# A fused two-layer attention and expert kernel: the output projection as seven block products

## The reference

```python
mixed = (gates[:, :, 0] * (out_a @ w_o_nsa[l]) + gates[:, :, 1] * (out_b @ w_o_mla[l])
         + gates[:, :, 2] * (out_c @ w_o_fox[l]))
x = x + mixed.astype(x.dtype) @ w_out[l]                 # [256,1024] @ [1024,1024]
x = x + hier_moe(rmsnorm(x, norm_ffn[l]), ...)           # logits, top group, top 2 experts, gate/up/down
```

## Time and profile before

| | us |
|---|---|
| three runs, median | 1014.33 |
| lowest, highest | 1013.62, 1015.16 |
| the profiled execution | 1014.46 |
| its span, first to last instruction | 1012.5 |
| TensorE busy in it | 936.8 (93%) |
| VectorE, ScalarE busy | 383.2, 241.6 |
| mean granted TensorE clock | 0.971 |

### The profile page before, as it was taken

The page is one execution under the profiler, slowest core; times in us unless marked ns, Lnnn a source line. Parts: engine busy times, 40 slices in busy tenths (PEclk is TensorE's granted clock), DMA queues, the critical chain, the costliest instruction groups (busy, mean ns, idle before and its releaser), DMA issues. The chain is left out here.

```text
span 1012.5 us, 14003 instructions
## 1 busy us (share of the span) xinstructions
PE 936.8 (93%) x5512; PEld 638.8 (63%) x5512; DVE 383.2 (38%) x1034; ACT 241.6 (24%) x682; POOL 78.6 (8%) x121
## 2 busy tenths in 40 slices
PE   9999999999999998677899999999999999986676
PEld 8888778775586543334288887887747855532342
DVE  2523676774633211111131337677565321100112
ACT  1211454552111020000111015655411202000002
POOL 0300000114000000000020000000220000000000
PEclk9999999999999998898999999999999999987899
DMA  9985655439989999999998443436398999999995
GB/s 291 299 271 143 139 168 160 167 99 316 333 353 361 421 420 421 422 421 421 359 311 268 130 149 111 143 100 220 122 358 310 351 402 417 420 422 420 421 415 186
DMA packets 137191, 295.14 MB, mean 291 GB/s; under 512 B 14158, under 2 KB 101412, under 8 KB 115620
## 3 DMA queue, kind: packets, MB, share of 16 engines
q1 hardware_dynamic: 132672, 289.41, 77.5%
q10 hardware_dynamic: 4452, 4.81, 2.5%
HBM read 291.56 MB, written 2.64 MB: 291 GB/s over the span
## 5 line engine op out<-in xcount | busy, mean ns | idle before, releaser
L2206 PE MATMUL bank<-ring,tail 128*32 128x512 f32 x896 | 113.5, 664 | 46.6 <-DMA ring<-in_moe_w_up 42.5
L1266 PE MATMUL bank<-ring,tail 128*128 128x256 f32 x672 | 156.3, 384 | 0.2
L1266 PEld LDWEIGHTS bank<-ring,tail 128*128 128x128 f32 x672 | 124.3, 190 | 24.5 <-issue 8.3
L1074 PE MATMUL bank<-tail,ring 128*128 128x256 f32 x512 | 112.6, 380 | 0.0
L2206 PEld LDWEIGHTS bank<-ring,tail 128*32 128x32 f32 x896 | 32.6, 121 | 123.3 <-issue 123.1
L1074 PEld LDWEIGHTS bank<-tail,ring 128*128 128x128 f32 x512 | 96.7, 190 | 13.3 <-issue 0.4
L2507 DVE SCALAR_TENSOR_TENSOR tail<-tail,bank 128x256 f32<-128x256 f32 x16 | 6.7, 422 | 232.1 <-ACT tail L2356 232.1
L1602 ACT ACTIVATE ring<-ring,small 128x128 f32<-128x128 f32 (+1 forms) x128 | 56.6, 444 | 77.4 <-DVE small L1896 77.4
L1428 PE MATMUL bank<-ring,tail 128*128 128x512 f32 x168 | 73.6, 594 | 0.0
L2263 PE MATMUL bank<-ring,tail 128*32 128x512 f32 x480 | 60.3, 610 | 7.7 <-DMA ring<-in_moe_w_down 4.1
L2213 PE MATMUL bank<-tail 128*128 128x512 f32 x128 | 59.2, 606 | 0.0
(11 more groups left out here) (334 smaller groups left out, 1155.5 us busy)
## 6 DMA issues: line engine op xcount, KB each, us to landing
ring<-in_moe_w_up SPq DMA_DIRECT2D x56, 1024.0 KB, 22.6
ring<-in_moe_w_gate SPq DMA_DIRECT2D x56, 1024.0 KB, 20.6
ring<-in_moe_w_down SPq DMA_DIRECT2D x52, 1024.0 KB, 15.2
ring<-in_w_in SPq DMA_DIRECT2D x47, 1024.0 KB, 9.0
ring<-in_w_out SPq DMA_DIRECT2D x8, 1024.0 KB, 8.5
ring<-in_moe_w_down SPq DMA_DIRECT2D x16, 512.0 KB, 15.9
ring<-in_moe_w_gate SPq DMA_DIRECT2D x14, 512.0 KB, 8.9
ring<-in_moe_w_up SPq DMA_DIRECT2D x14, 512.0 KB, 9.1
```

The lines of the kernel that those rows point to most:

```text
L1074: last = pe.matmul(dst, weight(k), hT[:, k, :], start=(k == 0), stop=(k == KD - 1))
L1266: last = pe.matmul(dst, tokens[:, k, :], weights[:, k, :], start=False, stop=(k == KD // 2 - 1), skip_group_check=True)
L2206: last = pe.matmul(bank[4][CAP * e:CAP * e + CAP, :].rearrange("p (a f) -> p a f", a=2), XT[:, k, CAP * e:CAP * e + CAP], ring[:, lo:hi + ...
```

## The change

The product of the 256 x 1024 mix and the 1024 x 1024 weights is split once in each direction: tokens a11, a12 (tile 0, chunks 0 to 3 and 4 to 7), a21, a22 (tile 1), weights left_top, left_low, right_top, right_low (512 x 512 each). Seven products of 128 x 512 x 512 take the place of eight, with sums and differences around them:

- The four loads of `w_out` are now the four 512 x 512 blocks.
- VectorE makes right_top - left_top as one operation of 2048 columns, placed ahead of the gated sum of branch block (4, 2). The three other weight differences are made in four chunks of 512 columns each.
- a21 is not copied by ScalarE; VectorE reads it from bank 3 for the token sums.
- The first product stays in bank 4, ScalarE copies it to bank 7, and the second is added in bank 4. The sixth and seventh and half of the fourth are added on in bank 7, which ScalarE copies to bank 4 and to bank 5 in between. Nine residual additions read what is complete.
- The transposes of tile 0 stand around the first step of the seventh product and `logits(0)` after its second step. `route(0)` on VectorE stands ahead of the additions of tile 1. Tile 1 goes through in chunks 4 to 7, 0 and 1, 2 and 3, all behind the last product, and ScalarE copies all of them.
- SyncE's loads wait for other events: c = 19 for the third product's differences, the first half row for the sixth product, 20 for the last left difference, 16 for the seventh product, 18 and the second half row for the end of the fourth.

```diff
-            i = n - L_OUT
-            whole(A["w_out"][layer].rearrange("(k p) n -> p k n", k=KD)[:, :, 256 * i:256 * i + 256])
+            right, low = divmod(n - L_OUT, 2)
+            w = A["w_out"][layer].rearrange("(k p) n -> p k n", k=KD)
+            sp.dma_start(ring[:, att_slot(n), :].rearrange("p (k n) -> p k n", k=4),
+                         w[:, 4 * low:4 * low + 4, 512 * right:512 * right + 512]).then_inc(done, 16)
...
+    Q1, Q2, Q5, Q3, Q6, Q7, Q4A, Q4B = 1, 2, 3, 3, 8, 9, 10, 11
...
-            sp.wait_ge(s_op, 4)
+            sp.wait_ge(s_tp, q_made(2, 3))
+            moe_load(sp, layer, 19)
+            sp.wait_ge(s_op, Q6)
             last_extra_row(sp, layer, 0)
-            for i, c in enumerate((16, 18, 19, 20)):
-                sp.wait_ge(s_op, 5 + i)
-                moe_load(sp, layer, c)
+            sp.wait_ge(s_tp, q_made(4, 3))
+            moe_load(sp, layer, 20)
+            sp.wait_ge(s_op, Q7)
+            moe_load(sp, layer, 16)
+            sp.wait_ge(s_op, Q4B)
+            moe_load(sp, layer, 18)
             last_extra_row(sp, layer, 1)
...
-            for i in range(4):
+            for i in range(3):
                 _kind, n, t, b = TURNED[i]
                 act.wait_ge(s_mxt, i + 1)
                 act.activation(mixT[:, t, 4 * n:4 * n + 4, :], ...).then_inc(s_mxe, 1)
+                if i == 1:
+                    act.wait_ge(s_op, Q1)
+                    act.wait_ge(s_mgd, row_done(4, 1))
+                    act.activation(bank[7][:, :], bank[4][:, :], ACT.Copy).then_inc(s_seed, 1)
...
             for kind, i in BLOCKS:
+                if (kind, i) == (4, 2):
+                    att_wait(dve, L_OUT)
+                    att_wait(dve, L_OUT + 2)
+                    dve.tensor_tensor(q_weights(2), q_weights(2), q_weights(0), ALU.subtract).then_inc(s_tp, 1)
...
+            first_product(range(4))
+            turn_mixed(pe, 1)
             out_piece(pe, 7, 2)
+            second_product((0, 1))
             out_piece(pe, 4, 2)
             turn_mixed(pe, 2)
+            second_product((2,))
             turn_mixed(pe, 3)
+            second_product((3,))
+            fifth_product()
+            third_product()
+            sixth_product()
+            pe.wait_ge(s_xa, 1)
             turn_x(0, 0, range(0, 4))
+            seventh_product((0,))
+            pe.wait_ge(s_xa, 5)
             turn_x(0, 1, range(4, 8))
+            seventh_product((1,))
             pe.wait_ge(s_wrg, 1)
             pe.wait_ge(s_xta, 1)
             pe.wait_ge(s_xtd, 1)
             logits(0)
+            seventh_product((2, 3))
+            fourth_product(0)
+            fourth_product(1)
             pe.wait_ge(s_xa, 6)
+            turn_x(1, 2, range(4, 8))
+            pe.wait_ge(s_xta, 2)
+            logits(1, range(4, 7))
             pe.wait_ge(s_msel, 1)
             pe.matmul(bank[0][:, 64:64 + NE], strict, Msel[:, 0, :], start=True, stop=True).then_inc(s_rk, 1)
             pe.wait_ge(s_xa, 8)
+            turn_x(1, 3, range(0, 2))
+            logits(1, range(7, 8))
+            pe.wait_ge(s_xa, 9)
+            turn_x(1, 1, range(2, 4))
             pe.wait_ge(s_xta, 3)
+            logits(1, range(0, 2))
+            pe.wait_ge(s_xta, 4)
+            logits(1, range(2, 4))
...
         def moe_scalar(act):
+            act.wait_ge(s_op, Q6)
+            act.wait_ge(s_xa, 1)
+            act.activation(bank[4][:, :], bank[7][:, :], ACT.Copy).then_inc(s_seed, 1)
...
+            dve.wait_ge(s_mxt, 4)
+            dve.wait_ge(s_mxe, 3)
+            dve.tensor_tensor(q_sum, a21, a22, ALU.add).then_inc(s_hs, 1)
+            dve.tensor_tensor(mixT[:, 1, 0:4, :], a11, a21, ALU.subtract).then_inc(s_hs, 1)
+            dve.wait_ge(s_op, Q1)
+            dve.wait_ge(s_hs, q_summed(3))
+            dve.tensor_tensor(a11, q_sum, a11, ALU.subtract).then_inc(s_hs, 1)
+            dve.wait_ge(s_op, Q2)
+            dve.wait_ge(s_hs, q_summed(2))
+            dve.tensor_tensor(a12, a12, a11, ALU.subtract).then_inc(s_hs, 1)
+            add_out(0, 0, 512, 4)
+            dve.wait_ge(s_op, Q5)
+            add_out(0, 512, 1024, 5)
+            add_out(1, 512, 1024, 5)
...
+            for k in range(4):
+                dve.wait_ge(s_op, Q3 + k + 1)
+                dve.tensor_tensor(right_low[:, k, :], right_low[:, k, :], right[:, k, :], ALU.subtract).then_inc(s_tp, 1)
...
+            third_difference(0)
+            third_difference(1)
+            dve.wait_ge(s_seed, q_copied(1))
+            add_out(0, 512, 1024, 4)
+            third_difference(2)
+            third_difference(3)
             dve.wait_ge(s_xt, 2)
             dve.tensor_copy(hT[:, 4:8, 0:P], bank[1][:, :].rearrange("p (k t) -> p k t", k=4)).then_inc(s_xtd, 1)
+            for k in range(4):
+                dve.tensor_tensor(left_low[:, k, :], left_low[:, k, :], right_low[:, k, :], ALU.subtract).then_inc(s_tp, 1)
             route(0)
```

More of the change, by code:

```diff
@@ L2097, in moe_tensor @@
         def moe_tensor(pe):
[L2100 to L2112 removed]
+            left_top, left_low, right_top, right_low = [q_weights(i) for i in range(4)]
@@ new lines, in moe_tensor, with steps, first_product @@
+            a11, a12, s3, a22 = mixT[:, 0, 0:4, :], mixT[:, 0, 4:8, :], mixT[:, 1, 0:4, :], mixT[:, 1, 4:8, :]
+            def steps(dst, tokens, weights, start, ks=range(4)):
+                for k in ks:
+                    last = pe.matmul(dst, tokens[:, k, :], weights[:, k, :], start=(start and k == 0), stop=(k == 3),
+                                     skip_group_check=True)
+                return last
+            def first_product(ks):
+                att_wait(pe, L_OUT)
+                pe.wait_ge(s_mxe, turned_mix(0, 0))
+                last = steps(bank[4][:, :], a11, left_top, True, ks)
+                if 3 in ks:
+                    last.then_inc(s_op, 1)
@@ new lines, in second_product, with fifth_product @@
+            def second_product(ks):
+                att_wait(pe, L_OUT + 1)
+                pe.wait_ge(s_mxe, turned_mix(1, 0))
+                pe.wait_ge(s_seed, q_copied(0))
+                last = steps(bank[4][:, :], a12, left_low, False, ks)
+                if 3 in ks:
+                    last.then_inc(s_op, 1)
+            def fifth_product():
+                pe.wait_ge(s_hs, q_summed(1))
+                pe.wait_ge(s_tp, q_top_done())
+                steps(bank[5][:, :], q_sum, right_top, True).then_inc(s_op, 1)
@@ new lines, in third_product, with sixth_product @@
+            def third_product():
+                att_wait(pe, L_OUT + 3)
+                pe.wait_ge(s_hs, q_summed(4))
+                for k in range(4):
+                    steps(bank[6][:, :], a12, right_low, True, (k,)).then_inc(s_op, 1)
+            def sixth_product():
+                pe.wait_ge(s_seed, q_copied(0))
+                for k in range(4):
+                    pe.wait_ge(s_tp, q_made(2, k))
+                    last = steps(bank[7][:, :], a11, right_low, False, (k,))
+                last.then_inc(s_op, 1)
@@ new lines, in seventh_product, with fourth_product @@
+            def seventh_product(ks):
+                pe.wait_ge(s_seed, q_copied(1))
+                for k in ks:
+                    pe.wait_ge(s_tp, q_made(3, k))
+                    last = steps(bank[7][:, :], s3, left_top, False, (k,))
+                if 3 in ks:
+                    last.then_inc(s_op, 1)
+            def fourth_product(half):
+                c = slice(256 * half, 256 * half + 256)
+                if half == 0:
+                    pe.wait_ge(s_xa, 4)
+                else:
+                    pe.wait_ge(s_seed, q_copied(2))
+                for k in range(4):
+                    pe.wait_ge(s_tp, q_made(4, k))
+                    last = pe.matmul(bank[6 + half][:, c], a22[:, k, :], left_low[:, k, c],
+                                     start=(half == 0 and k == 0), stop=(k == 3), skip_group_check=True)
+                last.then_inc(s_op, 1)
@@ new lines, in moe_vector @@
+            dve.wait_ge(s_op, Q1)
[8 more added lines that the diff above has]
+            add_out(1, 512, 1024, 5)
+            left, left_low, right, right_low = [q_weights(i) for i in range(4)]
```

116 lines of the change are left out of this document (53 added, 63 removed).

## The result

| | us |
|---|---|
| changed kernel, median of 21 runs (lowest to highest) | 1016.85 (1014.37 to 1018.59) |
| kernel before, median of 21 runs (lowest to highest) | 1013.63 (1012.5 to 1017.45) |
| ratio, 95% interval | 1.0026 (1.0018 to 1.0033) |
| profiled execution after, its span | 1017.26, 1015.5 |

By the ratio the change costs 0.26%, 2.6 us; the two medians are 3.2 us apart. The forecast was a cost of 1.0 us and a time of 1015.3, and its range, 1012.0 to 1017.6, holds the measured time. The times of the changed kernel lie in two groups: six within 1014.37 to 1014.95, and 14 of 21 above 1016. The first group is where the forecast's sum lies (1013.63 and 1.0 more); the second is what it did not put first.

A forecast was written before the change was run, and what follows sets the result against it. TensorE's output projection, through the hand-over of expert weight slots, was taken to set each layer's end; 34.2 us work plus 4.2 idle against 37.9 added 0.5 us in each of two layers, giving 1015.3 us, range 1012.0 to 1017.6.

The forecast's parts named there:

- The bound and the hinge: Hand-over to expert stage: first gate-up steps free weight slots, so each microsecond in tile 2's logits moves the layer equally.
- Rival (c): Expert loads: an earlier projection end is swallowed because loads were the bound all along; 1014.3 us, chance 0.08.
- The sum: Output projection: 34.2 us of work plus 4.2 idle against 37.9, so tile 2's logits end 0.5 us later per layer.
- transpose 3: TensorE in the projection: waits for VectorE's sum behind the 2048-column difference, going at 279.65 instead of 278.36, 1.29 us idle.
- its sign: What would show the forecast right: TensorE idles 4 us between 267 and 306, with the largest entry at transpose 3.
- The bounds: Range around the 0.5 us: waits -0.3, large difference up to +0.3, hand-overs +-0.8, giving -0.9 to +1.1 a layer.
- the fifth product's wait: Projection: the fifth product waits for the token sum, 0.69 minus one step of the second product, 0.19 us.
- GpSimd's norm factor: Before routing 2: GpSimd's last norm step ready 0.1 us before routing 2 begins, which is 0.2 us after tile 2's logits.
- rival (b): Whole projection: granted clock falls to 0.97, costing 1.5 us a layer, 1017.3 us; chance 0.23, shared with a longer chain.
- the gap of 0.55 us: Around the gather at 309.43 in the kernel before: clock stayed 1.00, taken as showing that short gaps are harmless.
- Rival (a): Projection: copies and large difference hidden, about 2 us idle left, 1.7 us a layer earlier, 1011 us; chance 0.14.
- the tail: End of the projection: transposes and ScalarE copies with no product beside them, idle of 0.95, then 0.30 and 0.24 us.

The follow-up runs named there:

- both moves together: Changed kernel with the 2048-column difference one block earlier and tile 2's first transposes between the fourth product's halves: 1010.28 us, ratio 0.9965; also called the last version.
- fourth profile: Changed kernel unaltered, profiled a fourth time: span 1012.7 us; gather to first gate-up step 5.28 us in layer 0, 6.57 in layer 1.
- third and fourth experiments: Changed kernel with tile 2's first transposes between the fourth product's halves, 1012.53 us; the same plus the 2048-column difference one block earlier, 1010.28 us.
- first profile of the changed kernel: Changed kernel unaltered, profiled with the result: span 1015.5 us; gather to first gate-up step 5.29 us in layer 0, 7.88 in layer 1.
- second experiment: Changed kernel with the 2048-column difference one block earlier on VectorE, ahead of the sum of branch block 7: 1013.76 us, ratio 0.9995.

## Why the prediction was right, point by point

**The bound and the hinge** held. The layer's end follows the first gate-up step: from there to the next layer it is 195.6 to 196.1 us in twelve of the traces, whichever kernel, and 197.2 and 197.4 in two, both with last down products that took longer. In layer 1 the way from the first gate-up step to the end is less fixed, 202.4 to 204.3 us, whichever kernel. The loads that went out 10 us earlier bought nothing. Rival (c) did not come to a test in the changed kernel, since there was no gain to swallow; in both moves together the gain of 1.6 us a layer was not swallowed.

**The sum** held. Predicted for layer 0: transpose 3 at 279.65, logits of tile 2 0.5 us later. Measured: 279.49, and 0.49 later. The large difference took 2.29 us. The step products waited for none of the twelve small differences. The idle of a wait plus the late start of the first matmul behind it was the right way to count: 0.69 listed as idle at 303.11 is 0.85 between what TensorE could have done and what it did. For the same reason its sign, 4 us of idle between 267 and 306, is not what the profile counts: it lists 2.4 us, and the rest stands in late starts. Layer 1 has the same 0.5: in the fourth profile, where the half clock began only after the logits, the gather comes 38.41 us after the first output product, before 37.90.

The bounds, though, do not follow from their terms. Eight waits of 0.1 are 0.8 and not 0.3, and with 0.3 and 0.8 the lower bound would be -1.1 and not -0.9. And one step is 0.43 us, so 0.69 less one step is 0.26 and not the 0.19 of the fifth product's wait; the rows show 0.18 there (26 records of 512 columns from 279.98 to 291.34). The sum stands, its path to that term does not.

**What was too small.** Routing 2 waited for GpSimd's norm factor (306.35), which I had put 0.1 us ahead of the logits. It costs 0.1 us a layer; in the third and fourth experiments routing 2 waits for the logits again, and the way from gather to gate-up is back at 5.19.

**What was priced wrong** is rival (b). I took the clock of a window in the expert stage, 0.97, as what less work on TensorE would cost over the whole projection, 1.0 us a layer, and gave it 0.23. What happened is the same cause in another shape: the clock is 1.00 in the projection itself and then goes to 0.50, for some 3 to 10 us, only after the last product. It costs 1.3 or 3.0 us where it falls, in 5 of 8 stages, 2.0 us an execution in the mean. That the rival's 1017.3 lies near the median of 1016.85 is luck: its price came from the clock of another stretch. So is part of the hit. The sum forecast 1.0 us and the order cost 1.2, but the change cost 2.6, and the measured time lies in the upper part of a wide range, 1.6 us above the forecast. The step that failed is the sentence that read the clock of 1.00 after the gap of 0.55 us in the kernel before as a sign that gaps are harmless. It showed that this stretch, as short as it was, kept the clock, and nothing about one that is longer: before, the last product ends at 303.35 and the first gate-up step begins at 310.75, 7.4 us; after, 301.8 and 311.3, 9.5 us with 0.69 us of idle more. I counted the move of the products to the front as 1.5 us of lost cover, and did not ask what TensorE is left with.

The Trainium skill (TensorE: Matmul & The Clock Gate, Why this matters for your kernels), which I weighed there, speaks of idle gaps, and by it the gaps here are short. The measurement decides: the clock fell with no entry of idle over 0.69 us between the last product and the fall. What the Trainium skill says elsewhere (Perfetto Trace Analysis, Matmul Optimizations), that matmuls should follow one another in batches because the engine scales its power with its use, points the way that this case went, as far as the clock tells it: 1.00 in the full stretches, 0.50 after the thin one. No run here shows power.

**Rival (a) and the reason for the change.** By the lengths of the records the seven products took 3.7 us a layer off TensorE's work. The stretch to the gather still grew by 0.5, so some 4.2 us went into idle and late starts. The two places that my sum put highest, transpose 3 and the tail, were worth 0.86 and 1.24 us a layer when undone, 4.2 us in two layers. The ratio to the kernel before fell by more, from 1.0026 to 0.9965, about 6.2 us. The 2.0 that are left fit the 2.0 of the falls and 0.2 of the norm factor; that no run of the last version has a fall is not shown.

## What to carry to other kernels

When work is taken from the engine that is full, walk the new order once instruction by instruction: the saving is only what is left after the new hand-overs, and the walk was right within 0.2 us here where the share of busy time said nothing. Keep a full-width product behind every transpose whose copy another engine must make; two small moves in the order turned a loss of 0.26% into a gain of 0.35%. After such a walk, find the stretches in which only narrow work is left, and read the granted clock there in several executions: one fall, at 1.3 or 3.0 us, cost more here than the 0.6 us by which the new order was longer in a layer. And when two executions are compared, count from the start of the stretch, not from the start of the program: the same kernel reached its projection up to 0.4 us earlier or later.

## What the runs showed of the hardware

- In the first profile of the changed kernel the clock fell to its half level after its last product of layer 1, in a stretch in which TensorE counts as busy for 3.21 of 4 us (799 to 803). Ahead of it stood four transposes, 0.69 us of idle, and logits of 40 columns. It stayed there for 10.2 us, until 812.8, within the first gate-up step. The four other falls of the changed kernel, and the one of the second experiment, lasted some 3.4 us and ended before that step.
- From the last output product to the first gate-up step it is 7.4 us before, 7.8 with the transposes between the halves of the fourth product, 8.6 with the old products in the new order: no fall in 6, 8 and 2 stages (in two of the 8 with one 256-column matmul more). With one unused 512-column matmul ahead of the logits it is 8.2 us from that matmul: none in 2. In the changed kernel and the second experiment it is 9.5 without a fall, and 6 of 10 stages have one. That the kernels without a fall never have one, or that the length alone decides, is not shown.
- It is not the same in each execution: the same kernel lost 0, 1.3 or 3.0 us in the same place.
- At half clock a record's length nearly doubles: the gather of 16 records took 3.76 against 2.03 us.
- ScalarE's copy from one bank to another took 0.58 to 0.59 us, the VectorE difference of 2048 columns 2.29, each as in the rows of before.
